# Hyena stage: context half of two sections ahead of the norm, low parts on VectorE, centre tap on ScalarE, lags together; causal blocks in the first attention

## The reference, cut to what matters

```
mask = kpos[None, :] <= qpos[:, None]
s = jnp.where(mask, s, jnp.finfo(jnp.float32).min)
p = jax.nn.softmax(s, axis=-1)
a = p[:, :, 0] - lam * p[:, :, 1]

u = centred_depthwise_conv(h @ w_in + b_in, short_w, short_b)
v, x1, x2 = jnp.split(u, 3, axis=-1)
filt = hyena_filters(L, w1, b1, w2, b2, w3, freq)
z = x1 * two_sided_fft_conv(v, filt[:, 0, 0], filt[:, 0, 1], filt_bias[0])
z = x2 * two_sided_fft_conv(z, filt[:, 1, 0], filt[:, 1, 1], filt_bias[1])
return z @ w_out + b_out
```

## Time and profile before

| | us |
|---|---|
| median of 3 runs | 2759.11 (2756.96 to 2761.08) |
| the profiled execution | 2759.9 |
| its span | 2758.1 |
| TensorE busy, 14502 matmuls | 2502.3 (91%) |
| VectorE busy | 1483.9 (54%) |
| ScalarE busy | 483.5 (18%) |
| GpSimd busy | 120.5 (4%) |

### The profile page before, as it was taken

How to read it: one execution, slowest core, us unless ns; L and a number is a source line. 1 busy time by engine, 2 the same in 40 slices (tenths; PEclk the granted TensorE clock), 3 DMA queues, 4 the chain that set the end, 5 groups by cost and what they waited for, 6 DMA issues and landing times.

```text
span 2758.1 us, 36937 instructions
## 1 busy us (share of the span) xinstructions
PE 2502.3 (91%) x14502; PEld 1711.1 (62%) x14502; DVE 1483.9 (54%) x2412; ACT 483.5 (18%) x918; POOL 120.5 (4%) x134
## 2 busy tenths in 40 slices
PE   7999999999999999997999789999998987877776
PEld 7997777999899588985766433333333763333233
DVE  6767554876876568766888723222225443112113
ACT  0003324100100231002221011111110532111111
POOL 1000000000000000003221100000000000000000
PEclk9999999999999998998999989999999998788888
DMA  7567643555556654564224579999997427999997
GB/s 251 188 221 270 236 135 102 180 184 195 170 184 212 251 177 166 183 257 128 61 61 160 221 303 422 422 422 422 422 422 303 174 81 327 422 422 422 422 422 308
DMA packets 234145, 712.29 MB, mean 258 GB/s; under 512 B 12645, under 2 KB 134517, under 8 KB 178624
## 3 DMA queue, kind: packets, MB, share of 16 engines
q1 hardware_dynamic: 223328, 676.37, 63.6%
q0 software_dynamic: 9856, 32.16, 3.3%
q10 hardware_dynamic: 864, 2.40, 0.2%
HBM read 708.69 MB, written 2.20 MB: 258 GB/s over the span
## 4 chain that ended last, share of the span: by engine, by line
PE 64%; DMA 23%; DVE 8%; issue 3%; ACT 1%; SPq 1%; POOL 0%; ACTq 0%; DVEq 0%; POOLq 0%
PE work L851 48%; PE acc L851 14%; DMA ring<-in_moe_down 12%; DMA ring<-in_moe_up 9%; PE work L867 2%; DMA ring<-in_ffn_w_in 1%; DMA ring<-in_ada_w 1%; SPq L711 1%; DVE stats L2286 0%; DVE scratch L2479 0%; DVE rows_h L2303 0%; DVE ring_parts L2146 0%; DVE scratch L2477 0%; DMA rows_x<-in_x 0%; DVE stats L2252 0%
## 5 line engine op out<-in xcount | busy, mean ns | idle before, releaser
L851 PE MATMUL work<-ring,scratch 128*64 128x512 f32 (+1 forms) x3008 | 560.2, 647 | 103.3 <-DMA ring<-in_moe_up 61.2
L851 PE MATMUL work<-rows_h_parts,ring_parts 128*128 128x256 f32 x3072 | 551.6, 286 | 18.2 <-DVE ring_parts L2139 8.4
L851 PEld LDWEIGHTS work<-rows_h_parts,ring_parts 128*128 128x128 f32 x3072 | 478.3, 195 | 22.7 <-issue 10.0
L851 PEld LDWEIGHTS work<-ring,scratch 128*64 128x64 f32 (+1 forms) x3008 | 146.6, 127 | 493.6 <-issue 283.8
L851 PE MATMUL work<-cols_x_parts,ring_parts 128*128 128x256 f32 x1536 | 415.3, 286 | 0.0
L2139 DVE TENSOR_TENSOR ring_parts<-ring,ring_parts 128x2048 fp32r<-128x2048 f32 x132 | 302.6, 2292 | 4.5
L851 PEld LDWEIGHTS work<-cols_x_parts,ring_parts 128*128 128x128 f32 x1536 | 288.1, 195 | 1.6
L851 PE MATMUL acc<-ring_parts,rows_h_parts 128*128 128x512 f32 x896 | 264.3, 391 | 0.0
L2688 DVE COPY scratch<-work 128x512 f32<-128x512 f32 x32 | 22.1, 691 | 368.8 <-PE work L851 368.8
L851 PE MATMUL work<-scratch 128*128 128x256 f32 (+4 forms) x1040 | 199.1, 379 | 6.4 <-issue 4.2
L851 PEld LDWEIGHTS acc<-ring_parts,rows_h_parts 128*128 128x128 f32 x896 | 165.1, 188 | 33.2 <-issue 1.0
(11 more groups left out here) (293 smaller groups left out, 2944.3 us busy)
## 6 DMA issues: line engine op xcount, KB each, us to landing
ring<-in_moe_down SPq DMA_DIRECT2D x128, 1024.0 KB, 25.9
ring<-in_moe_up SPq DMA_DIRECT2D x127, 1024.0 KB, 26.3
ring<-in_moe_gate SPq DMA_DIRECT2D x121, 1024.0 KB, 24.9
ring<-in_ffn_w_in SPq DMA_DIRECT2D x88, 1024.0 KB, 6.2
ring<-in_ada_w SPq DMA_DIRECT2D x48, 1024.0 KB, 9.5
ring<-in_ffn_w_out SPq DMA_DIRECT2D x44, 1024.0 KB, 6.0
ring<-in_xa_wkv SPq DMA_DIRECT2D x16, 1024.0 KB, 6.6
ring<-in_da_w_qkv SPq DMA_DIRECT2D x12, 1024.0 KB, 7.0
```

Of the source, the lines that this page charges most:

```text
L851: ins = nc.tensor.matmul(o, lhsT, rhs, start=start, stop=stop, **kw)
```

## The change

1. **Context half first.** `hyena_context_first(section)`, new, makes the context half (256 columns, plain fp32, 32 matmuls) of sections 0 and 1 of chunk 0 right behind `ffn(3)`, in columns 256 to 511 of the four `acc` banks. `hyena_project(0, 0)` and `(0, 1)` then make only the 256 latent columns, into the other half of those banks. `ada(3)`, its loads and its evacuation move behind the output projection, between the halves of `moe_norm0`. The context's low part (`ctx_low`) moves from `ffn(3)` to behind `mod_norm0`.
2. **Low parts.** GpSimd keeps blocks 0 to 3, and waits for `mod_norm0`'s rows before it starts; blocks 4 to 23 are made by VectorE (`hyena_lows`) in its own order.
3. **Centre tap.** ScalarE writes the centre tap, bias folded in (`hy_shift`), with a second ACTIVATE per tile; VectorE's L2477 goes.
4. **Lags together.** `filters(c, 0)` and `filters(c, 1)` stand together, the second in `acc`; both lags too. `conv(c, 2)` moves behind product(c, 0).
5. **Causal blocks.** Scores, exponentials, maximum and weighing take (j+1)*128 keys; the mask product takes the diagonal block alone.

```diff
+            def hyena_context_first(section):
+                n = plan["hy_w0"].loads + section
+                landed(n)
+                acc_at = plan["ffn3"].acc
+                pe.wait_ge(acc_read, NT * acc_at + section + 1)
+                w = slot(n, KB)
+                for a in range(2):
+                    o = acc[:, 2 * section + a, S:2 * S]
+                    for k in range(KB):
+                        mm(o, w[:, k, a * P:(a + 1) * P], cols_x[:, k, S:2 * S], k == 0, k == KB - 1,
+                           ctx_products_done if k == KB - 1 else None)
...
             ffn(3)
-            ada(3)
+            for section in range(2):
+                hyena_context_first(section)
...
+            ada(3)
             normed_to_cols("moe_norm0", rows_h, tiles=range(NT, 2 * NT))
...
-            for b in range(6 * (D // HC)):
-                c, section, a = b // 6, b // 2 % 3, b % 2
+            pool.wait_ge(rows_ready, plan["mod_norm0"].rows + NT)
+            for b in range(4):
+                pool.wait_ge(ctx_products_done, b + 1)
                 pool.wait_ge(hy_high_ready, b + 1)
...
                     elif c:
                         act.wait_ge(conv_ready, convs - 6 + (4 if section == 0 else 2) + a + 1)
...
+                    nc.scalar.activation(hy_y[:, 2 * section + a, :] if section < 2 else hy_x2[:, a, :], x, ACT.Identity,
+                                         bias=hy_shift[:, b:b + 1], scale=hy_cols[:, b, 3:4])
+                    nc.scalar.activation(hy_biased[:, 2 * (section % 2) + a, :], x, ACT.Identity,
+                                         bias=hy_cols[:, b, 0:1]).then_inc(read, 1)
...
-                    step(nc.vector.tensor_scalar(y, x, hy_cols[:, b, 3:4], hy_cols[:, b, 1:2], ALU.mult, ALU.add))
-                    step.settle()
...
                 for c in range(chunks):
                     hyena_kernel(c, 0, biases[0])
                     hyena_product(c, 0)
-                    hyena_lags(c, 1)
+                    hyena_conv(c, 2)
                     hyena_gate(c, 0)
+                    if c + 1 < chunks:
+                        hyena_lows(c + 1, 1)
                     hyena_kernel(c, 1, biases[1])
                     hyena_product(c, 1)
+                    if c + 1 < chunks:
+                        hyena_lows(c + 1, 2)
                     hyena_gate(c, 1)
                     if c + 1 < chunks:
                         hyena_conv(c + 1, 0)
                         hyena_conv(c + 1, 1)
-                        hyena_lags(c + 1, 0)
-                        hyena_conv(c + 1, 2)
+                        for o in range(2):
+                            hyena_lags(c + 1, o)
+                        if c + 2 < chunks:
+                            hyena_lows(c + 2, 0)
...
-                mm(o[:, 0:S], q_lo[:, h, j * P:(j + 1) * P], k_cols[:, h, :], True, False)
-                mm(o[:, 0:S], ident, mask[:, j, :], False, True)
-                mm(o[:, S:2 * S], q_hi[:, h, j * P:(j + 1) * P], k_cols[:, h, :], True, False)
-                mm(o[:, S:2 * S], ident, mask[:, j, :], False, True, signal)
+                w, own = (j + 1) * P, slice(j * P, (j + 1) * P)
+                for c, q in enumerate((q_lo, q_hi)):
+                    mm(o[:, c * S:c * S + w], q[:, h, own], k_cols[:, h, 0:w], True, False)
+                    mm(o[:, c * S + j * P:c * S + w], ident, mask[:, j, own], False, True, signal if c else None)
```

More of the change, by code:

```diff
@@ L298, in make_plan @@
     ffn(3)
-    norm("ffn_norm3", before=[ada(3)], cols=False)
+    norm("ffn_norm3", cols=False)
     norm("mod_norm0")
@@ L306, in project, with filters @@
                 plan.add(f"hy_w{c}", loads=3, convs=6)
-            plan.add(f"hy_p{c}{section}", tiles=2)
-    def filters(c, o):
+            plan.add(f"hy_p{c}{section}", tiles=2 if c or section == 2 else 0)
+    def filters(c):
         if c < chunks:
-            plan.add(f"hy_f{c}{o}", tiles=2, lags=NT)
+            plan.add(f"hy_f{c}0", tiles=2, lags=NT)
+            plan.add(f"hy_f{c}1", lags=NT)
     def turned(c):
@@ L320, in make_plan @@
     project(0, 1)
-    filters(0, 0)
+    filters(0)
     project(0, 2)
@@ L340, in make_plan @@
     for j in range(2 * NT):
+        if j == NT:
+            ada(3)()
         plan.add(f"moe_norm0_t{j}", tiles=2)
@@ L791, in _ @@
             ffn(3)
-            load_ada(3)
             def hand_over(n):
@@ L1248, in hyena_project @@
                             fin = bool(wp and k == KB - 1)
-                            mm(o, ws[wp][:, k, :], x[:, :, k, :], k == 0 and not wp and not xp, fin,
-                               tile_full[t % 4] if fin else None, done=done * int(fin and a == 1))
+                            mm(o, ws[wp][:, k, :], x[:, 0, k, :] if first else x[:, :, k, :], k == 0 and not wp and not xp, fin,
+                               full if fin else None, done=done * int(fin and a == 1))
                     t += 1
@@ L1344, in hyena @@
                         hyena_project(c + 1, 0, 0)
-                    hyena_filters(c, 1)
-                    if not more:
+                    else:
                         hyena_out_early(0)
@@ L1355, in hyena @@
                     if more:
-                        hyena_filters(c + 1, 0)
+                        for o_ in range(2):
+                            hyena_filters(c + 1, o_)
                         hyena_project(c + 1, 2, 1)
@@ L2034, in hyena_bias @@
                     t = plan[f"hy_p{c}{section}"].tiles + a
-                    filled(act, t)
+                    if c == 0 and section < 2:
+                        act.wait_ge(first_full, 2 * section + a + 1)
+                        x, read = acc[:, 2 * section + a, :], first_read
+                    else:
+                        filled(act, t)
+                        x, read = work[:, t % 4, :], tile_read[t % 4]
                     if section == 2:
                         act.wait_ge(conv_ready, convs + a + 1)
+                        if c:
+                            for q in range(2):
+                                read_out(act, plan[f"hy_y{c - 1}1"].tiles + q)
                     elif c:
@@ L2058, in hyena_odd @@
                 t = plan[f"hy_v{c}{o}"].tiles
+                act.wait_ge(lags_ready, plan[f"hy_f{c}1"].lags + NT)
                 for r in range(2):
@@ L2384, in da_weigh @@
                 step(nc.vector.tensor_tensor(s[:, 1:2], s[:, 1:2], lam[:, 0:1], ALU.mult))
-                first, second = probs[:, u % 2, 0:S], probs[:, u % 2, S:2 * S]
+                w = (u // DA_H + 1) * P
+                first, second = probs[:, u % 2, 0:w], probs[:, u % 2, S:S + w]
                 step(nc.vector.tensor_scalar(first, first, s[:, 0:1], None, ALU.mult))
@@ L2575, in hyena_gate, with hyena_lows @@
                     t += 1
+            def hyena_lows(c, section):
+                for a in range(2):
+                    b = hy_block(c, section, a)
+                    dve.wait_ge(hy_high_ready, b + 1)
+                    nc.vector.tensor_tensor(hy_w(ring_parts, c, section, a), hy_w(ring, c, section, a),
+                                            hy_w_high(b).bitcast(F32), ALU.subtract).then_inc(hy_low_ready, 1)
             def hyena(biases):
@@ L2859, in ctx_low @@
                 dve.wait_ge(ctx_high_ready, 1)
+                dve.wait_ge(ctx_products_done, 4)
                 nc.vector.tensor_tensor(hy_x_low[:, 1, :, :], cols_x[:, :, S:2 * S], hy_x_high[:, 1, :, :].bitcast(F32),
                                         ALU.subtract).then_inc(ctx_low_ready, 1)
-            ffn(3, between=ctx_low)
+            ffn(3)
             layer_norm("ffn_norm3", "ffn3", 2.0 * ALPHA, 4.0 * LN_EPS)
@@ L2869, in _ @@
                 cols_low(col_tile("mod_norm0", j, 0), j, hy_x_high[:, 0, :, :])
+            ctx_low()
             biases = [param_row(), param_row()]
```

92 lines of the change are left out of this document (66 added, 26 removed).

## The result

The changed kernel takes 2742.06 us (median of 4 runs, 2741.6 to 2745.43), the kernel before 2759.57 beside it: ratio 0.9937, 95% interval 0.9924 to 0.995: faster by 0.6%, clear of noise. The forecast was 2743.0. The profiled execution took 2742.14 us, span 2740.1 against 2758.1: 18.0 less.

| stretch | forecast | measured |
|---|---|---|
| first 303 us, same code | 0 | -0.8 |
| attention, first score to first output product: 40.1 to 33.3 | -6.5 | -6.9 |
| `ffn(3)` and before it | 0 | -0.2 |
| end of `ffn(3)` to the norm's second turn: 27.1 to 22.4 | -4.9 | -4.8 |
| first four blocks: 24.25 to 12.97 | -10.3 | -11.3 |

The account below looks back on a forecast made before the run. In the loop TensorE is nearly full and VectorE close behind, so waits between them decide. Terms -6.5 -4.9 -10.3 +1.9 +5.2 -1.5 sum to -16.1 us: 2743.0 against the median 2759.1, range 2731 to 2752.

Parts of the forecast that it names:

- Attention: Causal blocks in the attention: units of 1.7 and 2.15 us, VectorE full and TensorE with gaps; -6.5 us.
- GpSimd out of the norm: Norm behind ffn(3): VectorE's tiny operations no longer held up by GpSimd, second turn earlier; -4.9 us.
- Context half: First four blocks: context products hidden in the gap behind ffn(3), blocks 13.9 us instead of 24.2, still low clock; -10.3 us.
- rival 4: Context products behind ffn(3) not hidden, through doubled fp32 price or late weights: overrun 11 us, 2754; chance 0.05.
- Filters: Ahead of the loop's first turn: both filter orders now stand before section 2; +1.9 us.
- Loop: First turn to end of product(3, 0): period 63.4 us for chunks 1 and 2; +5.2 us, bounds -12.1 and +12.
- A: Loop interval from turn to end of product(c, 0): kernel waits for casts and low parts; 21.9 us, before 19.4.
- B: Loop interval from end of product(c, 0) to end of product(c, 1): conv, bias, casts, low parts, kernel, product; 22.8 us.
- C: Loop interval from end of product(c, 1) to the next turn: one filter more, 18.7 us, before 16.8.
- Rival 1: Loop's low parts hidden on VectorE, kernels start as early as before: period 57.6 us, total 2725.7; chance 0.12.
- ada(3): Moved into the gap ahead of the experts: clock up to -2, GpSimd's addition up to +1.2, evacuation +0.6; together zero.
- Rival 3: Experts start late: eight loads ahead of them in SyncE's queue uncovered, 19.2 us, total 2762.2; chance 0.05.

Follow-up runs that it names:

- the first experiment: Changed kernel with the first attention over all keys again, at full width, everything else as changed: 2751.35 us.
- fourth experiment: Changed kernel with ada(3), its loads, ScalarE's copy and GpSimd's addition back behind ffn(3), the context products behind it: 2742.39 us.
- second experiment: Changed kernel where GpSimd's first four low parts start once the context products are done, without waiting for the norm's rows: 2749.21 us.
- all moves: Changed kernel with section 2's taps ahead of the first kernel, low parts spread over lags, products and before the gate, casts behind their copies: 2731.62 us.
- fifth experiment: Changed kernel with the loop's low parts, all but the first four, back on GpSimd, nothing else undone: 2729.84 us, ratio 0.9881.

## Why the prediction was right, point by point

**Attention, -6.5 against -6.9.** Right in size, and in cause but for one sign: TensorE has gaps behind VectorE's rows, but VectorE isn't full (82% and 91%). Block 0 came to 1.54 us a unit (forecast 1.7), block 1 to 2.09 (2.15); the first experiment gives it all back.

**GpSimd out of the norm, -4.9 against -4.8.** Right, and shown: taking GpSimd's wait away brings back two holds of 2.25 and 2.08 us. The other 0.9 us came from `ada(3)`'s addition: with it back behind `ffn(3)` (fourth experiment) the row that took 1.06 us before takes 1.07 again.

**Context half, -10.3 against -11.3.** Free as said (rival 4 falls: 3.1 us of the gap were left). The size is off by one: I took 2.4 us for the low clock, and it cost 1.4: the first 16 matmuls took 3.29 us (1251.73 to 1255.02) instead of 1.92.

**Filters, +1.9 against +1.7**, and the first turn at 1281.8 forecast (with 6.5 of the attention), 1279.38 measured.

**Loop, +5.2 against +7.7**: the term that was mis-sized. The mechanism was right in each step (kernel at 6.86 behind the turn for 6.7, bias behind the taps, low parts behind the casts). A came to 22.7 and 22.2 for 21.9, B to 23.5 and 23.1 for 22.8, C to 18.5 for 18.7. Most of what the steps missed lies behind the kernels: "The two last v tiles wait for the kernel's release, which fits". It did not fit; TensorE waits 2.25 and 1.61 us, and the product's second half 0.67 us for ScalarE's copy of the last tile, so that products take 13.3 us for 13.05. Chunk 0's dip of the clock makes that wait 1.21 us and its product 13.8; it was foreseen nowhere. Together that is some 2 us. Another 1.7 lie ahead of the kernels (6.86 us for 6.7, 8.13 and 7.77 for 7.6) and in chunk 3 (19.7 for 19.3), and the kernels (2.0 for 2.1), C and rounding give 1.2 back. Of the 0.9 us by which chunk 0 is longer than the others, 0.5 is the dip: in the second experiment chunk 0 had none and still took 64.2. The upper bound of +12 does not follow from the interval losses that it names (A's 2.5 us nine times is over 22); nothing else was added up from it.

**Rival 1**, the low parts hidden, did not happen in the changed kernel, but the experiments come within 0.8 us of its period of 57.6: 59.6 with them on GpSimd, 58.4 with early taps as well. The Trainium skill (GPSIMD Engine Reference, 4.1 Engine selection) prefers VectorE for such work; the measurement decides otherwise, by 12 us, because the low parts and their wait for the casts stood on VectorE's path (kernel at 6.86 us behind the turn, 3.42 without them). The place counts beside the engine: with all moves and the low parts still on VectorE the period was 60.3.

**Last chunk, -1.5 against -1.2.** Right.

**ada(3), 0 against -1.3 up to the first expert, and -3.0 in it.** GpSimd's addition held VectorE for 0.87 us, inside the bound. The clock gave 1.6 behind the last product (32 matmuls in 3.84 us for 5.47), where TensorE's wait of 1.0 on VectorE went with it, and 3.0 in the first expert, above the bound of 2 that I set; 2.0 went again later. The fourth experiment shows that this is not a property of `ada(3)`: moving it back costs nothing, and in the run with the gaps filled, where it stood ahead of the experts, the same 64 matmuls took 16.8. That the sum came out within 1 us of the median is partly this: the loop's 2.5 too much and the clock's gain cancel.

**Rival 3**, uncovered expert loads, did not happen, though the reserve was nearly used up: DMA has about 1 us of idle left out of 14. It then sets the pace from the eighth expert on (29.8 us each for 27.4), and there the 20.0 us that TensorE was ahead by shrink to the 19 us that the loads are ahead by. The stream's next loads are issued when the first expert frees its slots, at 1593.12 against 1611.91, and that, not the eight loads, sets it.

## What to carry to other kernels

- Work on the engine whose result everybody waits for costs much of its length (here 4.2 us of 7.1 per chunk), even if another engine takes twice as long over it: give low parts to an engine that the profile shows idle, beside operations that it doesn't hold, and judge the move by the path, not by busy sums. VectorE's share of a chunk hardly tells the variants apart (83%, 80% and 82% at periods of 63.8, 59.6 and 58.4). A new place on the same path need not help: inside the products the same low parts gained nothing.
- Two moves in one loop (engine and place) are to be tried one at a time. Here the change held a gain of 34 us and a loss of 19 together (2760.09, 2744.66 and 2725.69), and the loop's period told so at once: 61.6 before, 63.8 after, 58.4 at best.
- Behind an added wait, ask also what the waiting engine releases next: the late v tiles were most of what the forecast missed.

## What the hardware showed that was not expected

**Which operations GpSimd holds.** In the traces with low parts on GpSimd, every VectorE operation that read an accumulator tile beside it (kernel, product's first rows, gate) had its own length, and those with two inputs in SBUF were held to the end of GpSimd's operation: 2.65 us for 0.75 in the taps, 2.25 for 0.16 in `newton` (second experiment). RECIPROCAL and TENSOR_SCALAR of 128x1 between them took 0.15. Two inputs are not the only way to be held: in the kernel before, the centre tap (L2477, a TENSOR_SCALAR of 128x512 with one input in SBUF) took 1.65 us beside GpSimd and 0.54 alone. The Trainium skill (SBUF — State Buffer, SBUF: two separate sides) describes a shared port pair that the first comer holds for its whole instruction, against VectorE operations with two SBUF inputs. The trace agrees for the operations with two inputs in SBUF. GpSimd is held in its turn: two low parts beside the context's low part took 6.77 us in the fifth experiment and 7.26 in the changed kernel instead of 4.7.

**A wait of 2.25 us can cost TensorE 1.3 us more.** Behind it TensorE ran for about 3.4 us at half clock in 10 of the 18 chunks (six runs) that had it, and the period grew by 0.5 to 1.7 us. There was no dip in the three chunks of the run with early taps, where the wait is 2.15, nor in the 12 chunks of the four runs with low parts on GpSimd, where it is 0.3. What tells a chunk with a dip from one without is not shown.

**Not every spread is the clock's.** The stretch from the last product to the next turn took 25.6 to 28.7 us from run to run. In three profiles of 14 the 32 matmuls behind that product ran at half clock (5.47 us for 3.84). The rest is a wait of TensorE for VectorE's evacuation of the output, 0 to 2.4 us, and VectorE there waits for a small load of `prow`: 0.97 us in the changed kernel's first profile, 2.06 in its second, 3.38 with the low parts inside the products. So a difference of 3 us between two profiles is no evidence for an edit, unless it lies in the stage that the edit touches and is larger than the spread of that stage.
